# Attention of a two-layer hybrid step: unsplit probabilities, an fp32 product with the values stationary, two heads in the halves of the array

## The chip, the cores and the metric

The kernel runs on one core of a Trainium2 chip. The metric is the device time of one execution in microseconds (us); each time given for a kernel is the median of several executions. The traces come from one profiled execution.

## What is computed

One step of a two-layer hybrid model over 640 tokens: 512 latent tokens (four tiles of 128) and 128 context tokens (one tile). Each layer has an input projection, an attention beside two smaller branches, an output projection and a mixture of experts. The part at issue is the attention:

```python
def block_attention(q, k, v):
    # H = 8 query heads, KV = 2 key/value heads, G = 4 query heads per key head, Dh = 64
    ...
    def one_block(qblk):
        s = jnp.einsum('bqkgd,bmkd->bkgqm', qblk, k).astype(jnp.float32) * scale
        p = jax.nn.softmax(s, axis=-1).astype(v.dtype)
        return jnp.einsum('bkgqm,bmkd->bqkgd', p, v)
    ...
```

Everything is fp32. Latent queries read 640 keys (four tiles of latent keys and one tile of cached keys), context queries read the 128 context keys. After the attention each of the three branches gets an RMS norm of its own; the merged 1024 columns go into the output projection.

## The kernel before

The kernel is written engine by engine, with every wait and its count by hand. Matrix products of full accuracy are made of fp32r (reduced fp32) parts: a tensor is split into a high part (a copy rounded to fp32r, on ScalarE) and a low part (the difference, on VectorE), and products of parts are accumulated.

The attention of a layer is one loop of 40 steps u = 8t + h: t runs over five token tiles in the order context, latent 0 to 3 (`ORDER`), h over eight heads. Tile t = 0 has one block of 128 keys, the others have five. TensorE in step u does, in this order:

1. the scores of head u: two products each (query parts against key parts) for 512 and 128 keys, into one of two PSUM slots (banks 0 and 1, or 2 and 3; L1421, L1422), once the exponentials of head u-2 are read out;
2. five transpositions of the probabilities of head u-1 into banks 4 and 5, of which there is one copy only (L1432), once the exponentials of u-1 are there and VectorE has read the transposed probabilities of u-2;
3. the product of head u-2 with the values into bank 6 (L1444 and L1446): for each block of keys the transposed high part of the probabilities (stationary, 128x128) against the value's two parts side by side (128 columns), then the low part against the value's high part (64 columns);
4. in the first two steps of a tile, transpositions of the next tile's queries (L1400), and in the steps that `ADA_AT` names (u = 10 to 15 and 26 to 31; two units in each of u = 10, 11, 26, 27, else one) a unit of the modulation's matrix product: four fp32 products with 32 stationary columns each, one in each quarter of the array's columns, 512 columns moving (L1314), whose weights come by a DMA of 1 MB into a ring of four.

ScalarE in step u copies the high part of the transposed probabilities of u-1 (`pTH`, L750), then takes the exponentials of u with their row sums (L758). VectorE takes the negated maximum of the scores of u (L1055) and then the low part of the transposed probabilities of u-1 (`pTL`, L1060). After every fourth head `o_low` (ScalarE, L723) and `o_high` (VectorE, L1032, L1033, L1036) add the two halves of the product and multiply by the reciprocal row sums; bank 6 is free for the next four heads when L1033 is done. Ahead of the loop the values of all six key tiles are split into `vv` (two copies on ScalarE, two subtractions on VectorE).

Other work that shares these engines: `split_hi` / `split_lo` of a projection weight in step 36; `branch_squares` (ScalarE, L737) and `normalise` (VectorE, L1044) of a finished token tile; `piece_add` (VectorE, L905) after the eighth and the sixteenth modulation unit, that is in steps 15 and 31. GpSimd first runs the convolution (six 128x1280 operations, L505 to L510), then `piece_out` (four small stores, L481), the loads of the next bias (L474), and `branch_stats` of the context tile (L516 to L518), on which `normalise(0)` waits in step 16.

Of the kernel before, what the change touches and what calls it, by code (L numbers as in the profile page):

```python
# [53 lines left out]
for _l in range(DEPTH):  # L54
# [15 lines left out]
    "v_hi": NKV, "v_lo": NKV, "k_hi": NKV, "k_lo": NKV, "kT_psum": NKEY, "kk": NKEY,  # L70
    "q_hi": NT, "q_lo": NT, "qT_psum": 2 * NT, "qT": 2 * NT, "scores": NT * NH, "nmax": NT * NH, "prob": NT * NH,
    "pT_psum": NT * NH, "pT_hi": NT * NH, "pT_lo": NT * NH, "pv": NT * NH, "o_low": 2 * NT, "o_read": 2 * NT,
    "attn_done": 2 * NT, "ss3": 3 * NT, "rstd3": NT, "mrg_ready": 3 * NT, "mT_psum": KD, "mT_hi": 2 * KD, "mT_lo": 2 * KD,
# [11 lines left out]
def build(nc, I, O):  # L85
    with ExitStack() as ctx:
# [86 lines left out]
        junk3 = pool[:, 11776:12288]  # L173
# [13 lines left out]
        piece = [misc[:, 0:N], frow[:, 0:N], frow[:, 0:N]]  # L187
        bpiece = [misc[:, N:2 * N], frow[:, N:2 * N], frow[:, N:2 * N]]
# [57 lines left out]
        def at(name, l, n):  # L246

            return l * PER_LAYER[name] + n
# [191 lines left out]
        def _(pl):  # L440
# [49 lines left out]
            for l in range(DEPTH):  # L490
# [10 lines left out]
                bias_in(l, 1)  # L501
# [32 lines left out]
                for t in range(3, NT):  # L534
                    branch_stats(t)

# [61 lines left out]
        def _(act):  # L598
# [27 lines left out]
            for l in range(DEPTH):  # L626
# [81 lines left out]
                for v in range(NKV):  # L708
                    act.activation(vv[v][:, :, 0:HD], kv[:, :, P + HD * v:P + HD * (v + 1)], ACT.Copy).then_inc(sem("v_hi"), 1)
# [9 lines left out]
                def o_low(g):  # L719

                    t, r = divmod(g, 2)
                    act.wait_ge(sem("pv"), at("pv", l, 4 * g + 4))
# [930 lines left out]
```

## Time and profile before

| | before |
|---|---|
| median of 3 runs (lowest, highest) | 1258.35 us (1257.8, 1263.3) |
| the profiled execution, its own time | 1263.37 us |
| its span, first to last instruction | 1261.4 us |
| attention of layer 1 of 2, first score to last normalised head | about 168 to 299 us of the span |
| attention of layer 2 of 2 | about 770 to 913 us |
| TensorE busy over the span | 1011.3 us (80%) |
| VectorE, ScalarE, GpSimd busy | 725.7, 609.4, 280.4 us |
| mean granted TensorE clock | 0.859 of 2.4 GHz |

TensorE's rows are matmuls (PE) and weight loads (PEld), which overlap; an fp32 product that is not fp32r shows as two weight loads and two matmuls. Where several matmuls stand as one row, "x5" is the number of their records. A granted clock of 1.00 is 2.4 GHz, 0.50 is 1.2 GHz.

### The profile page before, as it was taken

The page shows a single profiled execution, that of the slowest core. Times are in us where ns is not written, and L with a number is a line of the kernel's source. Part 1 is how long each engine was busy: PE and PEld are TensorE (multiplying, and loading weights), DVE is VectorE, ACT ScalarE, POOL GpSimd, SP SyncE. Part 2 cuts the span into 40 slices and gives each one's busy share as a digit, 9 for nine tenths or more (in the row PEclk, how much of TensorE's full clock was granted, in tenths as well). Part 3 has the DMA queues.
Part 4 walks back from the last instruction along what each step waited for, and adds up shares of the span by engine and source line. Part 5 has one row for each costly group of instructions (what it writes and reads, how often), then busy time and mean ns, then how long its engine had stood idle before and what let it go on. Part 6 is the DMA issues. An engine that isn't in the chain of part 4 may idle for free.

```text
span 1261.4 us, 14900 instructions
## 1 busy us (share of the span) xinstructions
PE 1011.3 (80%) x5192; PEld 816.4 (65%) x5192; DVE 725.7 (58%) x952; ACT 609.4 (48%) x904; POOL 280.4 (22%) x312
## 2 busy tenths in 40 slices
PE   3899978997988299998169997999889636999930
PEld 0588866876765078886148886787777535888720
DVE  0367055664434669997446704555533765999826
ACT  1652254654211168897265225544521224988822
POOL 3032052010241112120413305101002502112023
PEclk9999979996995589999569997959789657999965
DMA  9954018271316659998742301716213225999933
GB/s 329 282 213 161 8 46 293 79 256 56 121 67 235 231 211 404 418 413 294 258 165 70 113 30 46 273 54 245 90 34 117 87 96 198 395 411 419 372 134 153
DMA packets 85950, 248.33 MB, mean 197 GB/s; under 512 B 25644, under 2 KB 30252, under 8 KB 75656
## 3 DMA queue, kind: packets, MB, share of 16 engines
q1 hardware_dynamic: 72760, 209.54, 44.8%
q0 software_dynamic: 11696, 32.84, 7.6%
q10 hardware_dynamic: 1440, 5.24, 1.0%
q8 instruction: 32, 0.52, 0.2%
q14 instruction: 22, 0.18, 0.0%
HBM read 221.05 MB, written 30.21 MB: 199 GB/s over the span
## 4 chain that ended last, share of the span: by engine, by line
PE 65%; DVE 11%; DMA 9%; ACT 6%; issue 5%; POOL 4%; SPq 0%; POOLq 0%; ACTq 0%; DVEq 0%
PE ps L1297 11%; PE ps L1299 11%; PE ps L1298 10%; DMA pool<-in_moe_w 4%; PE ps L1304 4%; PE ps L1306 3%; PE ps L1305 3%; PE ps L1432 3%; PE ps L1444 3%; PE ps L1314 3%; PE ps L1446 2%; PE ps L1522 2%; PE ps L1421 2%; PE ps L1550 2%; PE ps L1422 2%
## 5 line engine op out<-in xcount | busy, mean ns | idle before, releaser
L1297 PE MATMUL ps<-wH,actH 128*128 128x512 f32 x608 | 248.5, 409 | 16.2 <-DVE actL L1245 12.0
L1299 PE MATMUL ps<-wH,actL 128*128 128x512 f32 x608 | 241.8, 398 | 0.0
L1298 PE MATMUL ps<-wL,actH 128*128 128x512 f32 x608 | 241.3, 397 | 0.0
L1165 DVE TENSOR_TENSOR wL<-raw,wH 128x2048 fp32r<-128x2048 f32 x64 | 146.0, 2284 | 11.3 <-ACT wH L804 10.6
L1297 PEld LDWEIGHTS ps<-wH,actH 128*128 128x128 f32 x608 | 117.5, 193 | 41.8 <-issue 13.3
L1299 PEld LDWEIGHTS ps<-wH,actL 128*128 128x128 f32 x608 | 116.8, 192 | 26.0
L1298 PEld LDWEIGHTS ps<-wL,actH 128*128 128x128 f32 x608 | 117.4, 193 | 22.9
L804 ACT ACTIVATE wH<-raw 128x2048 fp32r<-128x2048 f32 x64 | 122.0, 1910 | 4.1 <-DMA raw<-in_moe_w 4.1
L1304 PE MATMUL ps<-wH,actH 128*128 128x512 f32 x256 | 105.0, 410 | 4.7 <-DVE wL L1165 3.3
L1306 PE MATMUL ps<-wH,actL 128*128 128x512 f32 x256 | 101.4, 396 | 0.0
L1305 PE MATMUL ps<-wL,actH 128*128 128x512 f32 x256 | 101.1, 395 | 0.0
L565 POOL DMA_INDIRECT pool<-h2s,idxc x32 | 56.0, 1750 | 198.6 <-PE ps L1550 165.9
L750 ACT ACTIVATE actH<-ps 128x640 fp32r<-128x640 f32 (+1 forms) x80 | 49.5, 618 | 92.0 <-PE ps L1432 91.8
L1165 DVE TENSOR_TENSOR wL<-pool,wH 128x2048 fp32r<-128x2048 f32 x32 | 73.1, 2285 | 21.5 <-ACT wH L804 21.5
L1055 DVE TENSOR_REDUCE nmax<-ps 128x1 f32<-128x640 f32 (+1 forms) x80 | 57.1, 714 | 49.0 <-PE ps L1422 48.2
L1060 DVE TENSOR_TENSOR actL<-ps,actH 128x640 fp32r<-128x640 f32 (+1 forms) x80 | 57.2, 715 | 39.3 <-ACT actH L750 39.3
L1432 PE MATMUL ps<-ident,pool 128*128 128x128 f32 x336 | 62.0, 316 | 21.5 <-ACT pool L758 19.2
L1314 PE MATMUL ps<-raw,cpad 128*32 128x512 f32 x384 | 60.8, 731 | 21.8 <-DMA raw<-in_w_ada 21.8
L758 ACT ACTIVATE pool<-ps,nmax 128x640 f32<-128x640 f32 (+1 forms) x80 | 56.4, 705 | 25.3 <-DVE nmax L1055 25.1
L932 DVE TENSOR_TENSOR wL<-raw,wH 128x2048 fp32r<-128x2048 f32 x24 | 54.6, 2290 | 23.5 <-ACT wH L632 23.3
L819 ACT ACTIVATE actH<-ps 128x512 fp32r<-128x512 f32 x64 | 38.3, 598 | 56.4 <-PE ps L1550 53.9
L632 ACT ACTIVATE wH<-raw 128x2048 fp32r<-128x2048 f32 x24 | 45.9, 1931 | 38.4 <-PE ps L1299 38.4
(222 smaller groups left out, 1952.5 us busy)
## 6 DMA issues: line engine op xcount, KB each, us to landing
raw<-in_w_ada SPq DMA_DIRECT2D x48, 1024.0 KB, 6.7
raw<-in_moe_w SPq DMA_DIRECT2D x96, 512.0 KB, 7.4
raw<-in_w_in SPq DMA_DIRECT2D x16, 1024.0 KB, 8.4
raw<-in_moe_w SPq DMA_DIRECT2D x16, 1024.0 KB, 11.8
pool<-in_moe_w SPq DMA_DIRECT2D x32, 512.0 KB, 7.4
pool<-in_moe_w SPq DMA_DIRECT2D x16, 1024.0 KB, 10.4
ys<-pool SPq DMA_DIRECT2D x32, 512.0 KB, 10.7
pool<-modrow POOLq DMA_DIRECT2D x16, 512.0 KB, 5.1
```

What stands on the lines that cost most here:

```text
L804: act.activation(wH[:, i, :], mraw[parity][i], ACT.Copy).then_inc(sem(f"m_hi{i}"), 1)
L1055: dve.tensor_reduce(nmax[:, u % 2:u % 2 + 1], flat[:, 2 * N * (u % 2):2 * N * (u % 2) + keys], X, ALU.max, negate=True).then_inc(sem("nmax ...
L1060: dve.tensor_tensor(pTL[:, v % 2, 0:keys], flat[:, 4 * N:4 * N + keys], f32(pTH[:, v % 2, 0:keys]), ALU.subtract).then_inc(sem("pT_lo"), 1)
L1165: dve.tensor_tensor(wL[:, i, :], mraw[parity][i], f32(wH[:, i, :]), ALU.subtract).then_inc(sem(f"m_lo{i}"), 1)
L1297: pe.matmul(out, aH, wH[:, slot_, cols_], start=first, stop=False)
L1298: pe.matmul(out, aH, wL[:, slot_, cols_], start=False, stop=False)
L1299: return pe.matmul(out, aL, wH[:, slot_, cols_], start=False, stop=last)
L1304: pe.matmul(out, aH, hi, start=first, stop=False)
L1305: pe.matmul(out, aH, lo, start=False, stop=False)
L1306: return pe.matmul(out, aL, hi, start=False, stop=last)
L1314: m = pe.matmul(ps[32 * j:32 * j + 32, ada_bank(l, q), :], c32, raw[:, POS["ada", l, n] % RAWS, j * N:(j + 1) * N], start=(kt == 0), stop= ...
L1432: m = pe.transpose(ps[:, 4 + c // 4, (c % 4) * P:(c % 4) * P + P], prob[:, w % 2, c * P:(c + 1) * P], ident[:, :])
```

## The change

The probabilities are no longer split, and neither are the values. Heads are handled in pairs: step 2p handles head p' of the first key head and step 2p+1 the corresponding head of the second. The transposed probabilities of the even head are copied from PSUM by ScalarE, those of the odd head by VectorE, both in fp32 into `pT` (two buffers, one of them where the rotary tables were). In odd steps TensorE forms the product of a whole pair in fp32: the values are stationary (64 columns), the transposed probabilities move (128 columns), the first head's result goes to partitions 0 to 63 and the second's to 64 to 127 of bank 6. The result is the transposed output of two heads; ScalarE copies it out (`oT_out`), TensorE transposes it back into another part of bank 6 in the next even step, ahead of the transpositions of the probabilities, and VectorE multiplies it by the reciprocal row sums on its way to `mrg` (`pair_out`). `o_low`, `o_high` and the split of the values go.

Buffers move: `junk3`, `piece`, `bpiece` go into parts of `aux`. So on GpSimd `bias_in(l, 1)` waits for the end of the convolution and stands behind it, and the loads of `n2row` and of the first gate (`grow`) go from the middle of the attention to its end, the latter behind a wait for the last pair.

```diff
-        pTH = actH[:, 3072:4352].rearrange("p (b n) -> p b n", b=2)
-        pTL = actL[:, 3072:4352].rearrange("p (b n) -> p b n", b=2)
-        vv = [t[:, 4352:5120].rearrange("p (j n) -> p j n", j=NKEY) for t in (actH, actL)]
+        pT = [t.rearrange("p (v n) -> p v n", v=NKV) for t in (pool[:, 5120:6400], tabs[:, :, :, :, :].rearrange("p t a b d -> p (t a b d)"))]
+        oT = [pool[:, c:c + P] for c in (11520, 11648)]
...
                 if q == 1:
-                    pl.wait_ge(sem("k_final"), at("k_final", l, NT))
+                    pl.wait_ge(sem("conv_done"), at("conv_done", l, 1))
...
-                bias_in(l, 1)
                 tap = lambda w: cw[:, w, :].unsqueeze(1).to_broadcast([P, NT, 256])
...
+                bias_in(l, 1)
                 piece_out(l, 1)
                 bias_in(l, 2)
                 branch_stats(0)
-                pl.wait_ge(sem("conv_done"), at("conv_done", l, 1))
-                pl.dma_start(n2row, row(I["norm2"][l])).then_inc(sem("norm2_row"), 16)
-                pl.wait_ge(sem("piece_out"), at("piece_out", l, 64))
-                for c in range(2):
-                    pl.dma_start(grow[:, c, :], row(modrow[l][c, 2 * D:3 * D])).then_inc(sem("gate1_row"), 16)
...
                 for t in range(3, NT):
                     branch_stats(t)
+                pl.dma_start(n2row, row(I["norm2"][l])).then_inc(sem("norm2_row"), 16)
+                pl.wait_ge(sem("attn_done"), at("attn_done", l, 4 * NT))
+                for c in range(2):
+                    pl.dma_start(grow[:, c, :], row(modrow[l][c, 2 * D:3 * D])).then_inc(sem("gate1_row"), 16)
...
+                def oT_out(p):
+
+                    act.wait_ge(sem("pv"), at("pv", l, p + 1))
+                    if p >= 2:
+                        act.wait_ge(sem("oT_psum"), at("oT_psum", l, p - 1))
+                    act.activation(oT[p % 2], ps[:, 6, 0:P], ACT.Copy).then_inc(sem("oT"), 1)
...
-                for u in range(NT * NH + 1):
-                    if u >= 1:
-                        v = u - 1
-                        keys = 5 * P if v >= NH else P
-                        act.wait_ge(sem("pT_psum"), at("pT_psum", l, v + 1))
-                        if v >= 2:
-                            act.wait_ge(sem("pv"), at("pv", l, v - 1))
-                        act.activation(pTH[:, v % 2, 0:keys], flat[:, 4 * N:4 * N + keys],
-                                       ACT.Copy).then_inc(sem("pT_hi"), 1)
+                for u in range(NT * NH + 3):
+                    if u % 2 and u < NT * NH:
+
+                        w = u - 1
+                        keys = 5 * P if w >= NH else P
+                        act.wait_ge(sem("pT_psum"), at("pT_psum", l, w + 1))
+                        if w >= 4:
+                            act.wait_ge(sem("pv"), at("pv", l, w // 2 - 1))
+                        act.activation(pT[w // 2 % 2][:, 0, 0:keys], flat[:, 4 * N:4 * N + keys], ACT.Copy).then_inc(sem("pT"), 1)
+                    elif u % 2 == 0 and u >= 4:
+                        oT_out(u // 2 - 2)
...
+                def pair_out(p):
+
+                    t, r = divmod(p, 4)
+                    dst = mrg[:, ORDER[t], 0:512].rearrange("p (v r d) -> p v r d", v=NKV, r=4)[:, :, r, :]
+                    dve.wait_ge(sem("oT_psum"), at("oT_psum", l, p + 1))
+                    c = 2 * p % 16
+                    link(dve.reciprocal(rinv[:, 2 * r:2 * r + 2], rsum[:, c:c + 2]))
+                    dve.tensor_tensor(dst, ps[:, 6, P:2 * P].rearrange("p (v d) -> p v d", v=NKV), bc(rinv[:, 2 * r:2 * r + 2], HD),
+                                      ALU.mult).then_inc(sem("attn_done"), 1)
...
-                    if u >= 1:
-                        v = u - 1
-                        keys = 5 * P if v >= NH else P
-                        dve.wait_ge(sem("pT_hi"), at("pT_hi", l, v + 1))
-                        dve.tensor_tensor(pTL[:, v % 2, 0:keys], flat[:, 4 * N:4 * N + keys],
-                                          f32(pTH[:, v % 2, 0:keys]), ALU.subtract).then_inc(sem("pT_lo"), 1)
-                    if u >= 2 and (u - 2) % 4 == 3:
-                        o_high((u - 2) // 4)
+                    if u % 2 == 0 and 2 <= u <= NT * NH:
+
+                        w = u - 1
+                        keys = 5 * P if w >= NH else P
+                        dve.wait_ge(sem("pT_psum"), at("pT_psum", l, w + 1))
+                        if w >= 4:
+                            dve.wait_ge(sem("pv"), at("pv", l, w // 2 - 1))
+                        dve.tensor_copy(pT[w // 2 % 2][:, 1, 0:keys], flat[:, 4 * N:4 * N + keys]).then_inc(sem("pT"), 1)
+                    if u % 2 == 0 and u >= 4:
+                        pair_out(u // 2 - 2)
...
+                    if u % 2 == 0 and u >= 4:
+                        p = u // 2 - 2
+                        pe.wait_ge(sem("oT"), at("oT", l, p + 1))
+                        pe.transpose(ps[:, 6, P:2 * P], oT[p % 2], ident[:, :]).then_inc(sem("oT_psum"), 1)
...
-                    if u >= 2:
-
-                        w = u - 2
-                        t, h = divmod(w, NH)
-                        pe.wait_ge(sem("pT_lo"), at("pT_lo", l, w + 1))
-                        if w % 4 == 0 and w:
-                            pe.wait_ge(sem("o_read"), at("o_read", l, w // 4))
-                        slots = range(5) if t else [CTXK]
-                        o = (h % 4) * P
+                    if u % 2 and u >= 3:
+
+                        p = (u - 3) // 2
+                        pe.wait_ge(sem("pT"), at("pT", l, 2 * p + 2))
+                        if p:
+                            pe.wait_ge(sem("attn_done"), at("attn_done", l, p))
+                        slots = range(5) if p >= 4 else [CTXK]
                         for c, j in enumerate(slots):
-                            pe.matmul(ps[:, 6, o:o + P], pTH[:, w % 2, c * P:(c + 1) * P], vv[h // 4][:, j, :],
-                                      start=(c == 0), stop=False, skip_group_check=True)
-                            m = pe.matmul(ps[:, 6, o:o + HD], pTL[:, w % 2, c * P:(c + 1) * P], vv[h // 4][:, j, 0:HD],
-                                          start=False, stop=(c == len(slots) - 1), skip_group_check=True)
+                            for v in range(NKV):
+                                m = pe.matmul(ps[HD * v:HD * v + HD, 6, 0:P], kv[:, j, P + HD * v:P + HD * (v + 1)], pT[p % 2][:, v, c * P:(c + 1) * P],
+                                              start=(c == 0), stop=(c == len(slots) - 1))
                         m.then_inc(sem("pv"), 1)
```

## Rows read from the trace of the kernel before

**Rows 1.** The page: span; shares of the chain that ended last, by engine.

```profile
span 1261.4 us, 14900 instructions
PE 65%; DVE 11%; DMA 9%; ACT 6%; issue 5%; POOL 4%; SPq 0%; POOLq 0%; ACTq 0%; DVEq 0%
```

**Rows 2.** Windows: stretch, length, busy of PE PEld DVE ACT POOL, clock, DMA, GB/s.

```profile
168.00:186.00 18.00, 13.35 (x56) 11.63 (x57) 9.49 (x22) 9.78 (x33) 16.87 (x6) 0.53 0.02 4
190.00:211.00 21.00, 21.00 (x169) 14.06 (x169) 11.47 (x17) 10.94 (x26) 0.00 (x0) 1.00 0.86 315
815.00:852.00 37.00, 33.70 (x168) 32.00 (x168) 17.67 (x29) 17.09 (x38) 7.54 (x16) 0.62 0.25 84
```

**Rows 3.** Chain of waits, attention: start, length, what, number of records.

```profile
190.90 1.85 PE ps L1314 x16
...
201.33 0.57 PE ps L1432 x5
202.94 0.99 PE ps L1314 x8
...
204.77 0.57 PE ps L1432 x5
...
831.39 1.09 PE ps L1432 x5
...
835.78 1.09 PE ps L1432 x5
```

**Rows 4.** Timeline of one step with a modulation unit: start, length, engine, line.

```profile
200.43 0.19 PEld L1421 LDWEIGHTS ps<-actH,actL 128*128 128x128 f32 x1 [0.84 <-ACT pool L758]
...
201.13 0.53 PEld L1432 LDWEIGHTS ps<-ident,pool 128*128 128x128 f32 x5
201.36 0.82 DVE L1055 TENSOR_REDUCE nmax<-ps 128x1 f32<-128x640 f32 x1 [1.30 <-PE ps L1422]
201.63 0.19 PEld L1444 LDWEIGHTS ps<-actH 128*128 128x128 f32 x1
...
202.86 0.16 PEld L1314 LDWEIGHTS ps<-raw,cpad 128*32 128x32 f32 x8
```

**Rows 5.** Timeline of a step without one, at the full clock.

```profile
229.42 0.82 DVE L1060 TENSOR_TENSOR actL<-ps,actH 128x640 fp32r<-128x640 f32 x1 [0.49 <-ACT actH L750]
...
230.36 0.53 PEld L1432 LDWEIGHTS ps<-ident,pool 128*128 128x128 f32 x5
...
231.16 0.70 ACT L750 ACTIVATE actH<-ps 128x640 fp32r<-128x640 f32 x1 [1.00 <-PE ps L1432]
...
231.76 0.79 ACT L758 ACTIVATE pool<-ps,nmax 128x640 f32<-128x640 f32 x1
...
231.90 0.82 DVE L1060 TENSOR_TENSOR actL<-ps,actH 128x640 fp32r<-128x640 f32 x1 [0.64 <-ACT actH L750]
...
232.44 0.20 ACT L758 ACTIVATION_READ_ACCUMULATOR pool<-ps,nmax 128x1 f32 x1
```

**Rows 6.** Chain of waits: a full-accuracy fp32 product, 320 moving columns (two records).

```profile
163.63 0.54 PE ps L1390 x2
```

**Rows 7.** Groups of instructions, shapes apart: the nearest small ones.

```profile
L750 ACT ACTIVATE actH<-ps 128x128 fp32r<-128x128 f32 x16 | 4.4, 277 | 6.7 <-PE ps L1432 6.6
L1032 DVE RECIPROCAL rinv<-rsum 128x4 f32<-128x4 f32 x20 | 3.6, 178 | 10.2 <-ACT pool L723 10.2
```

**Rows 8.** Timeline: the same VectorE operation during the convolution and after it.

```profile
179.67 1.91 DVE L1036 TENSOR_TENSOR pool<-pool,rinv 128x256 f32<-128x256 f32 x1
...
204.39 0.42 DVE L1036 TENSOR_TENSOR pool<-pool,rinv 128x256 f32<-128x256 f32 x1
```

**Rows 9.** Timeline: VectorE's wait in step 16 for GpSimd.

```profile
217.48 1.01 DVE L1044 TENSOR_SCALAR pool<-pool,stat 128x512 f32<-128x512 f32 x3 [3.65 <-POOL stat L518]
```

**Rows 10.** Chain of waits: the last head's transpositions and the last output.

```profile
293.05 0.76 PE ps L1432 x5
...
298.91 0.44 DVE pool L1036
```

More of the change, by code:

```diff
@@ L69 @@
     "z_done": NT, "shifted": 96, "conv_done": 1, "front_used": 1, "sgT_psum": 1, "sgT_ready": 1, "sgu_psum": 4, "sgu_done": 4,
[L70 removed]
+    "k_hi": NKV, "k_lo": NKV, "kT_psum": NKEY, "kk": NKEY,
     "q_hi": NT, "q_lo": NT, "qT_psum": 2 * NT, "qT": 2 * NT, "scores": NT * NH, "nmax": NT * NH, "prob": NT * NH,
[L72 to L73 removed]
+    "pT_psum": NT * NH, "pT": NT * NH, "pv": 4 * NT, "oT": 4 * NT, "oT_psum": 4 * NT,
+    "attn_done": 4 * NT, "ss3": 3 * NT, "rstd3": NT, "mrg_ready": 3 * NT, "mT_psum": KD, "mT_hi": 2 * KD, "mT_lo": 2 * KD,
     "gate1_row": 32, "scale2_row": 32, "shift2_row": 32, "gate2_row": 32, "oproj_psum": 2 * NT, "oproj": 2 * NT,
@@ L759, in _ @@
                             accum_out=rsum[:, u % 16:u % 16 + 1]).then_inc(sem("prob"), 1)
-                    if u >= 2 and (u - 2) % 4 == 3:
-                        o_low((u - 2) // 4)
                     if u in W_AT:
@@ L774, in _ @@
                             q_hi(t + 2)
-                o_low(2 * NT - 1)
                 branch_squares(NT - 1)
@@ L1007, in _ @@
                                           ).then_inc(sem("z_done"), 1)
-                for v in range(NKV):
-                    dve.wait_ge(sem("v_hi"), at("v_hi", l, v + 1))
-                    dve.tensor_tensor(vv[v][:, :, HD:], kv[:, :, P + HD * v:P + HD * (v + 1)], f32(vv[v][:, :, 0:HD]),
-                                      ALU.subtract).then_inc(sem("v_lo"), 1)
                 def sgu_out(g):
@@ L1023, in _ @@
                     sgu_out(g)
-                def o_high(g):
-                    t, r = divmod(g, 2)
-                    dst = mrg[:, ORDER[t], 256 * r:256 * r + 256].rearrange("p (h d) -> p h d", h=4)
-                    dve.wait_ge(sem("o_low"), at("o_low", l, g + 1))
-                    c = (8 * t + 4 * r) % 16
-                    link(dve.reciprocal(rinv[:, 4 * r:4 * r + 4], rsum[:, c:c + 4]))
-                    dve.tensor_tensor(dst, ps[:, 6, :].rearrange("p (h s d) -> p h s d", h=4, s=2)[:, :, 0, :], dst,
-                                      ALU.add).then_inc(sem("o_read"), 1)
-                    dve.wait_ge(sem("o_read"), at("o_read", l, g + 1))
-                    dve.tensor_tensor(dst, dst, bc(rinv[:, 4 * r:4 * r + 4], HD), ALU.mult).then_inc(sem("attn_done"), 1)
+                def pair_out(p):
[6 more added lines that the diff above has]
+                                      ALU.mult).then_inc(sem("attn_done"), 1)
                 def normalise(t):
                     dve.wait_ge(sem("rstd3"), at("rstd3", l, t + 1))
-                    dve.wait_ge(sem("attn_done"), at("attn_done", l, 2 * t + 2))
+                    dve.wait_ge(sem("attn_done"), at("attn_done", l, 4 * t + 4))
                     for j, (a, b) in enumerate(((0, 512), (512, 768), (768, 1024))):
@@ L1047, in _ @@
                 q_lo(1)
-                for u in range(NT * NH + 1):
+                for u in range(NT * NH + 3):
                     if u < NT * NH:
@@ L1073, in _ @@
                         piece_add(l, 1 + PIECE_AT.index(u))
-                o_high(2 * NT - 1)
                 normalise(NT - 1)
@@ L1406, in _ @@
                 pe.wait_ge(sem("kk"), at("kk", l, NKEY))
-                pe.wait_ge(sem("v_lo"), at("v_lo", l, NKV))
+                pe.wait_ge(sem("kv_raw"), at("kv_raw", l, NT))
                 pe.wait_ge(sem("sgu_done"), at("sgu_done", l, 4))
-                for u in range(NT * NH + 2):
+                for u in range(NT * NH + 3):
                     if u < NT * NH:
-                        t, h = divmod(u, NH)
-                        v = h // 4
-                        if h == 0:
+                        t, s_ = divmod(u, NH)
+                        v, h = s_ % 2, s_ // 2 + 4 * (s_ % 2)
+                        if s_ == 0:
                             pe.wait_ge(sem("qT"), at("qT", l, 2 * t + 2))
```

21 lines of the change are left out of this document (6 added, 15 removed).

## The prediction

> **What bounds the kernel now.** I read the page first, then the granted clock and busy time of stretches of the attention, then the chain of waits, then single steps in the timeline. TensorE holds 65% of the chain that ended last [rows 1]. The change touches only the attention loops, some 131 us and 143 us long, so the question is what bounds a step there. There are three answers.
>
> Steps with a modulation unit (u = 10 to 15 and 26 to 31): TensorE is busy 21.00 of 21.00 us at the full clock [rows 2], and the transpositions of successive steps start 204.77 - 201.33 = 3.44 us apart [rows 3]. The weight loads mark one step [rows 4]: scores 200.43 to 201.13, 0.70 us; transpositions to 201.63, 0.50; product with the values to 202.86, 1.23; the unit 0.99 [rows 3]. The sum is 3.42: TensorE has no slack.
>
> Steps without one, at the full clock: these follow a loop through three engines. The transpositions start at 230.36, ScalarE's high copy at 231.16, VectorE's low part at 231.90; it lasts 0.82 and the next transpositions wait for it, as those at 230.36 did for the low part of 229.42 to 230.24 [rows 5]. That is 0.80 + 0.74 + 0.82 + about 0.1 = 2.46 us, just above TensorE's own 0.70 + 0.50 + 1.23 at most.
>
> Steps at the lower clock: in layer 2, 815 to 852, the clock is 0.62 on average, TensorE is busy 33.70 of 37.00 us [rows 2], and steps are 835.78 - 831.39 = 4.39 apart [rows 3]: TensorE again.
>
> **Part by part**, per pair of latent heads, with a full-clock row unless said.
>
> Product. Before: 2 x 1.23 = 2.46. It has 5 x (128 + 64) x 2 = 1920 columns, 0.80 us at 2.4 GHz, so columns are not its price; its 20 matmuls each wait for a 128-column load, some 0.11 apart. The new one has ten fp32 products of 128 columns. An fp32 product of 320 columns takes 0.54 us [rows 6], which is 4.05 cycles a column at 2.4 GHz, so one of 128 takes 0.213. Whether the two halves run side by side the trace shows in quarters: a second modulation unit adds 1.85 - 0.99 = 0.86 [rows 3] for four products of 512 columns, where one alone would take 4 x 512 / 2.4 = 0.853. Four ran in the time of one, and their weight loads vanish behind them. So the pair takes 5 x 0.213 = 1.07. What one unit takes beyond 0.86 is 0.13, the change into and out of the split array; I add it once. Taken: 1.2, with 0.05 for the next loads, 1.25. Bounds: 1.07 from the same rows, and 10 x 0.213 + 0.13 = 2.26 if the halves queue. I take the low side because the quarters are the same mechanism.
>
> The Trainium skill (TensorEngine Tiling (Array Packing), Key Properties) says that changing the tiling mode drains TensorE. It speaks against the change, which adds two mode changes per pair; the unit's 0.13 agrees with it. By that rule, with 0.13 due at each of the two, 32 pairs give back 4 us more than by one; the page has no figure of its own.
>
> Back-transposition: one matmul like the five that take 0.50 [rows 4], so 0.10, taken as 0.15; bounds 0.1 and 0.9, the latter if TensorE sits through the copy (0.28 like L750's 128x128 [rows 7], plus its latencies). In a step with a unit the copy is hidden by unit and scores (1.7 us), in others by the scores alone (0.70).
>
> VectorE: two low parts of 0.82 become one copy of the same 640 elements, 0.82 by L1060 [rows 5]; `pair_out` is a reciprocal of 0.18 and a product of some 0.28 [rows 7], as much per pair as `o_high` was. VectorE has 2 x 0.82 + 0.82 + 0.5 = 3.0 of work per pair. ScalarE: two high copies become one of 0.70 and one of 0.28. Neither engine bounds.
>
> Pairs with units: 2 x 0.70 + 2 x 0.50 + 1.25 + 0.15 + 2 x 0.99 = 5.78 against 6.88, 1.10 less. Six such pairs a layer, 12 in all: **13 us**.
>
> Pairs without, at the full clock. The old loop goes; late next is a longer one: exponentials 0.88 [rows 5] + 0.05, transpositions 0.50, pair product 1.25, scores of the next even head until their maximum starts 0.93 (200.43 to 201.36 [rows 4]), maximum 0.82 + 0.04: 4.47 against 4.9, or 5.2 with the 0.6 that `o_low` and `o_high` add to each fourth step. Two other paths tie with it: VectorE's copy of the odd head frees banks 4 and 5, and its `pair_out` frees bank 6, within 0.1 us of need. Ties seldom line up, so I take 4.7 and 0.5 a pair, bounds 0 and 0.75. Of the 20 pairs without units, 8 ran like this by the spacing of L1432 in the chain (six in layer 1, two in layer 2): **4 us**.
>
> Pairs at the lower clock, another 8, six of them in layer 2: a step takes 4.39 [rows 3] where TensorE's parts at the full clock sum to 2.40, a factor of 1.83; the new pair's 2 x 1.20 + 1.25 + 0.15 = 3.80 becomes 6.95, which I take as 7.2 against 8.78, and 1.4 won after ties: **11 us**. The last 4 are held in steps 16 and 36 by waits that stay (below): 0.5 each, **2 us**.
>
> Context tile: one block of keys, lower clock (0.53 [rows 2]); product and copies shrink little and two stages join, so 0, bounds -2 and +2. One thing is won: L1036, both inputs in SBUF, took 1.91 instead of 0.42 while GpSimd ran the convolution [rows 8]; `pair_out` reads PSUM, like L1055, which did not stretch. **3 us** in two layers.
>
> Tail: from the last transpositions at 293.05 to the end of the last output, 298.91 + 0.44, are 6.3 us [rows 10]. After: 0.8, VectorE's copy 0.83, the product 2.3, copy, back-transposition and `pair_out` 1.3: 5.3. **2 us** in two layers.
>
> At nothing: the split of the values, since the last score keys and queries came later (cover: TensorE's transpositions of keys; without it some 2 us a layer). On GpSimd `bias_in(1)` moves behind the convolution, 2 us of issue and one landing: its reader is `piece_add` in step 15, over 20 us later. `piece_out`, `bias_in(2)` and `branch_stats(0)` keep their order, so VectorE's wait of 3.65 us in step 16 [rows 9] stays. The second-norm and gate loads move to the end of the attention, behind `branch_stats` of the last tile; their readers come after a whole projection half, 30 us on. Uncovered, they would cost some 5 us a layer. Modulation weights arrive at 315 GB/s with the DMA busy 0.86 [rows 2]; a faster step asks for 1 MB per 2.9 us instead of 3.44, 360 GB/s, where 315 / 0.86 gives 366: it just fits, with four units ahead in the ring.
>
> Sum: 13 + 4 + 11 + 2 + 3 + 2 = 35. The 0.13 for the split array may fall due on the way in and on the way out, which is 4 us more in 32 pairs; I take off half of that: 33. The profiled execution took 1263.4 (span 1261.4 and 2 around it), so it would take 1230; the median shown is 5 lower, and I forecast **1225**, by itself 1215 to 1237.
>
> **Rivals.**
> - The clock rises sooner. Layer 2's second latent tile ran at the lower clock for most of its length [rows 2, 3], layer 1's at the full one by 229 us [rows 5], after the same stall; the new product keeps TensorE on columns rather than on weight loads. Four or five pairs at 4.7 instead of 7.2: 11 us more, 1214.
> - The clock stays low through both tiles without units, in both layers, because TensorE waits more often. Six pairs at 5.2 become 7.2 instead of 4.7: 15 us lost, 1240.
> - The round trip is exposed: TensorE stands in order behind ScalarE's copy in each even step, 0.6 a pair in 32 pairs, 19 us: 1244. For it speaks that ScalarE does the copy only after the odd head's exponentials; against it, the scores between.
> - Slower: the halves take turns, so the change doesn't do what it says. Then a pair's product is 2.26: 1.07 more in each of 32 latent pairs and twice that in the 12 at the lower clock, so 32 + 12 = 44 times 1.07 is 47, less some 4 where TensorE has slack in the loop, 43: 1268. It decides where 44 times the surplus is 33, at a product of 1.25 + 0.75 = 2.0 us. Against it stand the quarters of rows 3. The Trainium skill (FP8 and Floating Point Precision, TensorE Precision Notes) gives true fp32 as four passes through the array, which the 4.05 cycles a column agree with; it says nothing on halves.
>
> **How the numbers follow.** Chances: forecast 0.47, sooner clock 0.15, low clock 0.14, exposed round trip 0.10, halves in turn 0.14. A difference of 0.5%, 6.3 us, is about what a measurement here can tell from none. Faster: 0.47 + 0.15 + 0.09 + 0.05 = 0.76; within: 0.05 + 0.05 + 0.01 = 0.11; slower 0.13. The range leaves out the halves in turn and little else: 1207 to 1254.
>
> **What would show it.** Right: pair products in which the two halves start within 0.05 us of one another and that last 1.1 to 1.3 us at the full clock; pairs with units 5.7 to 6.0 apart; no TensorE wait for `oT` above 0.2 us; L1036's 1.9 us gone. Wrong: a product of 2 us or more, or modulation steps bound by DMA. The sum is wrong too if the stall of step 16 grows by what the steps before it save, or if the granted clock of the tiles without units differs from that of before.

## The result, and the profile after

| | before | after |
|---|---|---|
| median (lowest, highest), side by side | 1260.82 us (1257.8, 1267.8) | 1221.21 us (1219.96, 1224.83) |
| ratio of the medians, 95% interval | | 0.9683 [0.9634, 0.9732] |
| the profiled execution, its own time | 1263.37 us | 1220.32 us |
| its span; mean granted clock | 1261.4 us; 0.859 | 1218.5 us; 0.886 |

The forecast was 1225 us, in a range of 1207 to 1254: the time lies 3.8 us under the forecast. The profiled executions differ by 43.0 us. The table below takes the attention of each layer apart at the first exponential of each token tile; the last column ends with `normalise` of the last tile, some 4.4 us behind the last head's output. Tiles latent 0 and latent 2 hold the modulation units, latent 1 and 3 have none.

| us | context | latent 0 | latent 1 | latent 2 | latent 3 to end | sum |
|---|---|---|---|---|---|---|
| before, layer 1 | 15.4 | 27.6 | 27.5 | 28.0 | 35.4 | 133.8 |
| before, layer 2 | 15.4 | 28.6 | **35.4** | 30.2 | 36.1 | 145.7 |
| after, layer 1 | 13.9 | 25.3 | 24.9 | 26.2 | 31.0 | 121.3 |
| after, layer 2 | 13.9 | 25.7 | 25.1 | 26.2 | 30.9 | 121.7 |

So 36.5 of the 43.0 us are in the attention, 10.3 of them in one tile. Another 6.5 lie where no code changed: from the start of the last `h2` ahead of layer 1's router to the cast of the router's index lists it takes 32.8 us before and 26.3 after (called the router stage below). The first question is therefore whether these two places belong to the change at all.

The chain of waits of the kernel after, a pair of heads with modulation units (start, length, what, records); it answers to [rows 3]. L1436 is the new product, L1303 a unit, L1425 the transpositions of the probabilities.

```profile
197.99 1.24 PE ps L1436 x20
199.23 0.99 PE ps L1303 x8
...
201.19 0.55 PE ps L1425 x5
201.74 0.99 PE ps L1303 x8
...
204.14 1.24 PE ps L1436 x20
```

The product of two heads takes 1.24 us, the pair 204.14 - 197.99 = 6.15 where it took 6.88. The timeline of TensorE's weight loads in the same stretch (start, length, engine, line, shapes, idle time just before in brackets) shows what the 1.24 consists of; it answers to [rows 4]:

```profile
200.86 0.14 PEld L1416 LDWEIGHTS ps<-ident,pool 128*128 128x128 f32 x1
200.92 0.58 PEld L1425 LDWEIGHTS ps<-ident,pool 128*128 128x128 f32 x5
201.67 0.16 PEld L1303 LDWEIGHTS ps<-raw,cpad 128*32 128x32 f32 x8 [0.17 <-issue]
...
203.37 0.53 PEld L1425 LDWEIGHTS ps<-ident,pool 128*128 128x128 f32 x5
204.06 1.07 PEld L1436 LDWEIGHTS ps<-pool 128*64 128x64 f32 x20 [0.17 <-issue]
205.31 0.16 PEld L1303 LDWEIGHTS ps<-raw,cpad 128*32 128x32 f32 x8 [0.17 <-issue]
```

The loads of the pair's twenty matmuls (ten fp32 products, two records each) take 1.07 us, the forecast's figure to the digit. What stands beside it is the 0.17 in brackets: each time the array goes into another form (whole to halves at 204.06, halves to quarters at 205.31, whole to quarters at 201.67) the loads stand still for 0.17 us, three times in a pair with units.

By the loads, the pair is two scores of 0.70, transpositions of 0.69 and 0.75 with the gap behind them, the product of 1.25 with the gap behind it, a back-transposition of 0.06 and two units of 0.99: 6.13 in sum.

### The profile page after: what moved, and what is told of

It is laid out like the page before. It is cut to its first block, busy times and chain, and to the rows that moved or that the text cites. A ratio compares the mean times of both kernels' runs of the same rounds, so it can differ in the third digit from the quotient of the medians.

```text
span 1218.5 us, 14984 instructions
## 1 busy us (share of the span) xinstructions
PE 960.8 (79%) x5232; PEld 753.8 (62%) x5232; DVE 686.8 (56%) x928; ACT 585.6 (48%) x880; POOL 282.5 (23%) x312
## 4 chain that ended last, share of the span: by engine, by line
PE 59%; DVE 13%; DMA 11%; ACT 7%; issue 5%; POOL 4%; SPq 1%; POOLq 0%; ACTq 0%; DVEq 0%
PE ps L1286 11%; PE ps L1288 11%; PE ps L1287 10%; PE ps L1293 3%; PE ps L1295 3%; PE ps L1294 3%; PE ps L1303 3%; PE ps L1425 3%; DMA raw<-in_moe_w 3%; DMA pool<-in_moe_w 3%; PE ps L1436 2%; PE ps L1410 2%; ACT wH L799 2%; DVE wL L1154 1%; PE ps L1540 1%
## 5 line engine op out<-in xcount | busy, mean ns | idle before, releaser
L1286 PE MATMUL ps<-wH,actH 128*128 128x512 f32 x608 | 248.2, 408 | 17.3 <-DVE actL L1234 13.2
L1303 PE MATMUL ps<-raw,cpad 128*32 128x512 f32 x384 | 57.8, 697 | 21.8 <-DMA raw<-in_w_ada 21.8
L799 ACT ACTIVATE wH<-pool 128x2048 fp32r<-128x2048 f32 x32 | 61.2, 1911 | 4.8 <-DMA pool<-in_moe_w 4.8
L1540 PE MATMUL ps<-ident,pool 128*128 128x128 f32 x256 | 39.9, 282 | 29.0 <-DMA pool<-h2s,idxc 29.0
L1425 PE MATMUL ps<-ident,pool 128*128 128x128 f32 x336 | 57.3, 299 | 6.1 <-ACT pool L756 4.9
```

Of the source, the lines that this page charges most:

```text
L799: act.activation(wH[:, i, :], mraw[parity][i], ACT.Copy).then_inc(sem(f"m_hi{i}"), 1)
L1286: pe.matmul(out, aH, wH[:, slot_, cols_], start=first, stop=False)
L1303: m = pe.matmul(ps[32 * j:32 * j + 32, ada_bank(l, q), :], c32, raw[:, POS["ada", l, n] % RAWS, j * N:(j + 1) * N], start=(kt == 0), stop= ...
L1425: m = pe.transpose(ps[:, 4 + c // 4, (c % 4) * P:(c % 4) * P + P], prob[:, w % 2, c * P:(c + 1) * P], ident[:, :])
```

## The experiments

**Do the halves run side by side?** The first kernel issues all products of one half before those of the other:

```diff
-                        for c, j in enumerate(slots):
-                            for v in range(NKV):
+                        for v in range(NKV):
+                            for c, j in enumerate(slots):
```

> The changed kernel with the ten fp32 products of a pair in another order: all five of the first half, then all five of the second, so that neighbours share a half of the array and can't run side by side. Nothing else differs. Theory (the gain is TensorE's time for the product, and it hangs on the two halves running together): a pair's product goes from 1.24 to about 2.2 us at the full clock, each of 32 latent pairs gets about 1 us longer, and the time rises from 1221 to 1250 to 1262, which is the old kernel's. Rival (the gain is the shorter chain through ScalarE and VectorE, and the product lies beside it): under 10 us, at most 1231. Second rival (two products of one half overlap as well): no change.

Measured: 1245.32 us (1240.5 to 1249.57), ratio to before 0.9875 [0.9812, 0.9938]. Its chain of waits:

```profile
200.65 1.95 PE ps L1436 x20
202.60 0.99 PE ps L1303 x8
```

In turn the product takes 1.95 instead of 1.24, so the halves do run side by side in the changed kernel. The medians are 24.1 us apart, but not all of that is the product's: the attention tiles grew by 17.1 us in sum, and the router stage, whose code is the same, stood at 33.2 instead of 26.3. The 0.71 would be 23 us in 32 latent pairs; the pairs that are held at steps 16 and 36 did not get longer (in layer 1 their products start 10.23 and 8.62 us behind those ahead, against 10.46 and 8.90). The time is under the range expected for this reason, and because the product in turn takes 1.95 and not about 2.2: why products of one half take less than their sum is open.

**What does the back-transposition cost where it stands?** Here it is moved behind the transpositions of the probabilities:

```diff
-                    if u % 2 == 0 and u >= 4:
-                        p = u // 2 - 2
-                        pe.wait_ge(sem("oT"), at("oT", l, p + 1))
-                        pe.transpose(ps[:, 6, P:2 * P], oT[p % 2], ident[:, :]).then_inc(sem("oT_psum"), 1)
                     if 1 <= u <= NT * NH:
...
                         m.then_inc(sem("pT_psum"), 1)
+                    if u % 2 == 0 and u >= 4:
+                        p = u // 2 - 2
+                        pe.wait_ge(sem("oT"), at("oT", l, p + 1))
+                        pe.transpose(ps[:, 6, P:2 * P], oT[p % 2], ident[:, :]).then_inc(sem("oT_psum"), 1)
```

> The changed kernel with the back-transposition of a pair behind the transpositions of the probabilities in TensorE's order, instead of ahead of them. Theory: TensorE's waits for ScalarE's copy (23 us in 16 waits in the trace of the changed kernel) lie mostly where TensorE waits for VectorE or GpSimd anyway, and only some 0.1 to 0.2 us in pairs without units are lost: 1216 to 1221. Rival (the round trip is exposed, 0.6 us a pair): 1200 to 1206. If the pair's output gets late instead, so that the next product waits for bank 6: slower, up to 1230.

Measured: 1214.98 us (1212.86 to 1218.12), ratio 0.9648 [0.9593, 0.9702]: 6.2 us less than the changed kernel, just under what the theory expected. The changed kernel was not run beside it and the two ratios' intervals overlap, but no execution of the one (1219.96 and up) reaches the other's, and in the traces the attention fell from 243.0 to 235.7 us in sum. The waits of TensorE in the changed kernel, 190 to 240 us, say where (waiter, releaser, us in total, times, longest):

```profile
PE ps L1416 <- ACT pool L721: 4.9, 3, 4.2
```

and its chain where step 16 has been held:

```profile
214.05 0.74 DVE nmax L1043
...
216.08 0.29 ACT pool L721
216.41 0.48 PE ps L1416
216.89 1.07 PE ps L1425 x5
```

In a step that is held, the exponentials come late, ScalarE's copy of the product comes behind them, and TensorE stands before the back-transposition although the probabilities are there: from the maximum at 214.05 to the transpositions at 216.89 it takes 2.84 us. With the block moved, this is 1.70:

```profile
215.10 0.74 DVE nmax L1043
...
216.80 1.30 PE ps L1421 x5
```

(L1421 is the same transposition there.) In steps that run freely nothing changed: pairs with units are 6.15 apart in both kernels (198.97 to 205.12 with the block moved), pairs without 4.68 and 4.67 (224.59 to 229.27, and 224.41 to 229.08). The tiles say the same: latent 1 went from 24.9 and 25.1 to 23.7 and 23.4, latent 3 from 31.0 and 30.9 to 30.0 and 30.1, latent 2 fell by 0.8 and the context tile by 0.4 in each layer, latent 0 rose by 0.3 in one layer and fell by 0.5 in the other.

**The stall of step 16 and the clock.** In both kernels step 16 waits for `normalise(0)`, and that for GpSimd, which first does four stores and four loads:

```profile
206.44 0.70 DVE pool L900
...
207.42 2.01 POOL modrow L481 x4
209.50 2.02 POOL pool L474 x4
212.13 0.88 POOL stat L517
213.44 0.61 DVE pool L1032 x2
```

(chain of the kernel after). From the end of `piece_add` to the last two of the three operations of `normalise(0)` are 213.44 - 207.14 = 6.3 us, as they were before (211.58 to 217.88). Two kernels take this away by doing `branch_stats(0)` ahead of `piece_out(l, 1)` and `bias_in(l, 2)`, one made from the kernel before, one from the kernel after:

```diff
+                branch_stats(0)
                 piece_out(l, 1)
                 bias_in(l, 2)
-                branch_stats(0)
```

> The kernel before with one line moved on GpSimd: the statistics of the context tile ahead of the small stores and loads of the modulation, which removes VectorE's wait of 3.65 us in step 16 and with it TensorE's longest idle time in the attention. Theory (the granted clock falls in that idle time, and in layer 2 of the kernel before it stayed low for the whole next tile): the second latent tile of layer 2 falls from 35.4 us to about 23, that of layer 1 from 27.5 to 22, in all 15 to 18 us: 1243 to 1246. Rival (the clock of that tile has other causes than this stall): only the stall itself goes, 6 to 8 us: 1253 to 1255.

> The changed kernel with the same line moved. Theory: the stall is 3.5 to 4 us a layer here too, and a few us at the lower clock behind it go as well: 1209 to 1214. Against the kernel before with the line moved this gives the worth of the change without the help of the clock: if 10 us of the change's 40 were the clock of one tile, the two kernels with the moved line lie about 30 apart; if the clock had no part, about 40.

Measured: 1244.12 us (1240.17 to 1250.63), ratio 0.9884 [0.9819, 0.995], and 1214.08 us (1212.03 to 1216.21), ratio 0.9634 [0.9579, 0.9689]. They are 30.0 us apart, as expected if the clock has a part, where the kernels before and after are 39.6 apart. The granted clock of latent 1 in windows (stretch, length, busy of PE PEld DVE ACT POOL, clock, DMA share, GB/s), first the kernel before, layer 2, then the kernel before with the statistics first, layer 1:

```profile
820.00:824.00 4.00, 1.14 (x8) 0.94 (x9) 3.44 (x9) 2.25 (x5) 1.53 (x3) 0.99 0.53 181
824.00:850.00 26.00, 26.00 (x115) 24.84 (x114) 12.10 (x17) 10.90 (x26) 1.25 (x3) 0.50 0.11 37
```

```profile
218.00:222.00 4.00, 3.97 (x34) 3.67 (x32) 3.23 (x6) 2.81 (x5) 1.06 (x2) 1.00 0.47 158
222.00:226.00 4.00, 3.62 (x28) 3.20 (x27) 2.75 (x5) 2.37 (x5) 0.00 (x0) 1.00 0.79 266
```

TensorE is busy 1.14 of 4 us in the stall, then the clock is at its lower level (1.2 GHz) although it is busy all the time. Without the stall the clock stays at 2.4 GHz throughout latent 1, and this tile takes 22.1 us in both layers of the one, 19.3 in both of the other. The attention takes 130.3 and 129.2 us against 117.5 and 117.7: the change is worth 24.3 us in the attention when neither kernel meets the stall of step 16. A second stall, in step 36, stays in both, and the clock falls behind it in both (0.50 over 282 to 296 us of the one and 269 to 275 of the other, layer 1), so latent 3 is not free of the clock in this comparison.

**Does the lower clock belong to the kernel?** Both kernels once more, unaltered, for their traces:

> The kernel before once more, for its trace alone. If the granted clock goes with the kernel: second latent tile 27.5 us in layer 1 and 35.4 in layer 2, router stage of layer 1 32.8 us. If it differs between executions of one kernel: the second latent tile of layer 2 at 26 to 28 us, or that of layer 1 at 35, and a router stage of 27 us can come.

> The changed kernel once more, for its trace alone. If the granted clock goes with the kernel: attention tiles within 0.3 us of the first trace (layer 1 13.9, 25.3, 24.9, 26.2, 31.0; layer 2 13.9, 25.7, 25.1, 26.2, 30.9) and the router stage of layer 1 (last h2 to the lists) 26.3 us. If it differs between executions of one kernel: second latent tile of one layer up to 33 us, router stage 33 us.

Measured, one execution each: 1251.28 us and 1224.05 us, 27.2 apart where the first traces are 43.0 apart. The kernel before, the same code, has 29.6 us in latent 1 of layer 1 (27.5 in the first trace) and **26.65** in layer 2 (35.4), and 27.0 in the router stage (32.8). Its windows in layer 2:

```profile
817.00:821.00 4.00, 0.96 (x8) 0.78 (x7) 2.63 (x6) 1.35 (x4) 2.02 (x4) 1.00 0.48 158
821.00:825.00 4.00, 3.73 (x21) 3.33 (x20) 3.19 (x7) 2.40 (x5) 0.51 (x1) 0.67 0.77 261
825.00:829.00 4.00, 4.00 (x32) 3.87 (x31) 2.23 (x4) 2.23 (x5) 0.00 (x0) 0.91 0.03 12
```

The same stall, the same work, and the clock is at its lower level for some 3.4 us (8 us x (0.33 + 0.09)) instead of some 30 us, from 824 to about 854. The four traced stalls of the kernel before order the tile by this stretch: some 3.4 us low go with 26.65 us in latent 1, 6.8 with 27.5, 10.2 with 29.6 and 30 with 35.4. The layers of one execution differ as much as the executions do. So how long the lower clock lasts is not fixed by the code. The kernel after repeated itself: all tiles within 0.4 us of the first trace, the router stage 27.3 us. In its windows (first trace, layer 1) the clock falls too, and stays low for some 6.8 us, as it does in both layers of both its traces:

```profile
213.00:217.00 4.00, 0.59 (x3) 0.59 (x4) 2.48 (x5) 2.18 (x6) 0.01 (x1) 0.66 0.11 36
217.00:221.00 4.00, 4.00 (x22) 3.48 (x22) 2.52 (x5) 1.35 (x5) 0.00 (x0) 0.50 0.02 4
221.00:225.00 4.00, 3.48 (x34) 2.98 (x31) 2.17 (x5) 1.95 (x6) 0.00 (x0) 0.99 0.00 0
```

The router stage swings with the granted clock too. Its logits' products in the two traces of the kernel before (timeline: start, length, engine, line, shapes; below them the window of 21 us around them), first trace, then second:

```profile
392.49 3.60 PE L1522 MATMUL ps<-rw,pool 128*128 128x20 f32 x16
399.67 3.60 PE L1522 MATMUL ps<-rw,pool 128*128 128x20 f32 x16
...
384.00:405.00 21.00, 18.30 (x95) 13.82 (x91) 11.98 (x6) 2.83 (x3) 1.00 (x2) 0.57 0.79 273
```

```profile
395.15 2.19 PE L1522 MATMUL ps<-rw,pool 128*128 128x20 f32 x16
399.18 1.96 PE L1522 MATMUL ps<-rw,pool 128*128 128x20 f32 x16
...
387.00:408.00 21.00, 20.31 (x136) 15.56 (x136) 12.47 (x9) 3.50 (x4) 0.64 (x2) 0.74 0.91 306
```

Over all traces of this study the stage of layer 1 took between 26.3 and 33.2 us, with the same code there; variants of the kernel after met the long one too. The Trainium skill (TensorE: Matmul & The Clock Gate, Part 1) says that the gate's window runs free of the kernel, and that the number of products at the lower clock when a kernel starts therefore varies between runs of one kernel. That 35.4 and 26.65 us stand for the same tile agrees with it in kind; the sentence speaks of the start of a kernel, and why one stretch lasted 30 us no run here shows.

**How much of the old time was the low part?** The kernel before, without the products of the low part of the probabilities; the low part itself is still computed and waited for:

```diff
                             pe.matmul(ps[:, 6, o:o + P], pTH[:, w % 2, c * P:(c + 1) * P], vv[h // 4][:, j, :],
...
-                            m = pe.matmul(ps[:, 6, o:o + HD], pTL[:, w % 2, c * P:(c + 1) * P], vv[h // 4][:, j, 0:HD],
```

> The kernel before without the five products of the low part of the probabilities per head (64 columns each): that part of the output is left out, the low part itself is still computed and waited for. TensorE's share of a head's product falls from about 1.23 to 0.7 us, nearly what the change saves on TensorE (2.46 to 1.24 a pair), while VectorE's chain and the waits stay. Theory (where TensorE has no slack its time is the gain; elsewhere the chain is): the steps with a modulation unit go from 3.44 to about 2.9 and 24 of them give 12 to 13 us, steps without one at the full clock stay at 2.46, those at the lower clock fall from 4.39 to about 3.9: 1238 to 1246 in all. Rival (TensorE's time is all of it): as much as the change, 1218 to 1226.

Measured: 1229.78 us (1229.0 to 1231.44), ratio 0.9745 [0.9708, 0.9781], between the two cases. Tiles with units fell by 3.3 to 3.4 us each against the second trace of the kernel before, 13.4 in sum, where 12 to 13 were expected; latent 1 of layer 1 fell from 27.5 in the first trace, with a stretch at the lower clock as long, to 27.15 only. Where TensorE bounds the step the product counts, where the loop of the two copies bounds it, it doesn't. That is the theory's picture. Its 1238 to 1246 was missed by 8 us: latent 1 of layer 2 stood at 26.5 instead of the first trace's 35.4 and the router stage at 27.3 instead of 32.8, and these 14.4 us would bring it to 1244. With half the products left out a pair with units takes 2 x 2.91 = 5.82 (transpositions at 196.33, 199.24, 202.15); the change, with the whole product, takes 6.15.

**Three other arrangements of the pair.** The first puts the product into the even step behind the scores, ScalarE's copy behind its exponentials, and the back-transposition and `pair_out` into the next odd step; the second does this with the statistics first; the third leaves the product where it is and moves the modulation units from even into odd steps.

```diff
-                    if u % 2 and u >= 3:
+                    if u % 2 == 0 and u >= 4:
-                        p = (u - 3) // 2
+                        p = (u - 4) // 2
```

```diff
-none, third = (0,) * NH, (0, 0, 2, 2, 1, 1, 1, 1)
+none, third = (0,) * NH, (0, 0, 0, 4, 0, 2, 0, 2)
```

> The changed kernel with the product of a pair one step later, behind the scores of the next even head, the copy of its result behind that head's exponentials, the back-transposition and pair_out in the odd step after. It takes the product out of the loop that bounds pairs without units (exponentials, transpositions, product, scores, maximum). Theory: those pairs fall from about 4.7 us to TensorE's own time, 1.4 + 1.1 + 1.25 + 0.2 = 3.95, some 14 pairs, and the late back-transposition gives what it gave alone (6): 1203 to 1210. Rival (the two other paths that tie, VectorE's copy and pair_out, hold the pair at 4.5): 1213 to 1216, as with the late back-transposition alone. If the clock falls because TensorE now waits elsewhere: slower than 1221.

> The same with the statistics of the context tile ahead of the small stores on GpSimd as well, so without the stall of step 16. Theory: the two gains add, as they touch different tiles for the most part: 7 us below the kernel without that line, 1196 to 1203. Rival: with the shorter pairs the stall is what is left of several waits and going without it gives 10 or more; or the late product has already filled it, 0 to 3.

> The changed kernel with the modulation units of two steps put together behind a pair's product in the odd step (0, 0, 0, 4, 0, 2, 0, 2 for 0, 0, 2, 2, 1, 1, 1, 1), so that TensorE goes once less into and out of the split array in each pair with units; the number of units and of products is the same. Theory (each entry costs 0.17 us of idle weight loads and each leaving about 0.13): pairs with units go from 6.13 to about 5.85, 12 pairs, 3 to 4 us: 1217 to 1219. Rival (the entries are hidden): 1221. If the longer block of units delays the scores of the next head beyond what VectorE and ScalarE have in store: slower, 1224 or more.

Measured: 1224.27 us (1219.59 to 1230.23), 1216.97 (1216.64 to 1217.07) and 1229.15 (1228.23 to 1229.6). All three miss the ranges of their theories. The first won 4.6 us in the attention (238.4 against 243.0 in sum) and met 33.1 us in the router stage, so what puts its median above 1221 is not the attention, where its third case looked for it. The second lies 7.3 us under the first, the difference that was expected. In pairs without units its chain shows a new loop in place of the old:

```profile
219.96 1.31 PE ps L1422 x20
221.28 0.71 PE ps L1433 x5
222.01 0.84 DVE tabs L1051
222.98 0.75 PE ps L1433 x5
223.75 0.71 ACT pool L747
224.50 1.31 PE ps L1422 x20
```

(L1422 is the product there, L1433 the transpositions.) Banks 4 and 5 hold one head's transposed probabilities; with the product in between, transposition, copy, transposition, copy, product stand one behind the other, 4.54 us instead of 4.68. The scores have left the chain, and next to nothing is won. Its units, moreover, ran into their weights once:

```profile
188.35 7.00 DMA raw<-in_w_ada
```

The third came out in its slower case (1224 or more): it shows the price of a change of form and what avoiding it costs. Its chain:

```profile
199.73 1.24 PE ps L1436 x20
200.97 1.85 PE ps L1303 x16
...
203.69 0.83 DVE nmax L1043
...
206.25 1.24 PE ps L1436 x20
```

Two units in a row save one change (1.85 against 2 x 0.99), but the pair takes 6.52 instead of 6.15: behind product and both units the scores come late, and maximum, exponentials and transpositions follow them on the chain with TensorE idle. Spread over both steps, as in the change, the units cover that latency.

**Both gains together.** The changed kernel with the back-transposition moved and the statistics first:

> The changed kernel with both edits: the back-transposition behind the transpositions of the probabilities, and the statistics of the context tile ahead of the bias loads on GpSimd. Alone they gave 1221.2 - 1215.0 = 6.2 and 1221.2 - 1214.1 = 7.1 us. Theory: they are won in different places (6.2 in the pairs, 7.1 in step 16), so they add: 1206 to 1210, attention of a layer 113 to 115 us. Rival: both end in the same wait (a tile that comes sooner to step 16 only waits longer for GpSimd, or the clock rises later): 1211 to 1215, attention 116 to 118 us.

Measured: 1208.0 us (1206.08 to 1210.46), ratio to before 0.9596 [0.9539, 0.9652]. The attention takes 113.0 and 113.4 us, latent 1 is 19.1 in both layers, and the windows (latent 1 of layer 1) show why:

```profile
207.00:211.00 4.00, 3.91 (x40) 3.32 (x39) 3.12 (x8) 2.89 (x7) 3.80 (x8) 1.00 0.98 376
211.00:215.00 4.00, 3.48 (x35) 3.03 (x35) 3.01 (x6) 2.85 (x7) 0.03 (x1) 1.00 0.27 79
```

No stall in step 16, and no fall of the clock in latent 1; behind step 36 it still falls. The two gains of 6.2 and 7.1 by the medians add up to 13.2, as the theory had it. In the traces the attention fell by 16.5 us, where the two edits alone gave 7.3 and 7.7, and the router stage stood at 30.1. This version beats both kernels.

## Why the prediction was right, and where it was not

**The product: right.** 1.25 us were taken, 1.24 measured. The argument from the quarters in [rows 3] and the fp32 product in [rows 6] gave 1.07 for the loads of the pair, and 1.07 it is.

**The split form: mis-sized.** The step "What one unit takes beyond 0.86 is 0.13, the change into and out of the split array; I add it once" was wrong in number more than in size. The price is 0.17, and it falls due at each change of form that the trace shows a gap for: into the product, from product to unit, and from transpositions to unit in the even step, where the transpositions now come directly ahead of it. The transposition blocks therefore take 0.69 and 0.75 us by the loads, with the gap behind them (203.37 to 204.06, 200.92 to 201.67), and not 0.50. A pair with units takes 6.15, not 5.78; it won 0.73, not 1.10, which is 8.8 us in 12 pairs and not 13. The prediction weighed a second change at 4 us in all and took off half of that; the 0.37 in 12 pairs are 4.4. The Trainium skill (TensorEngine Tiling (Array Packing), Key Properties) says that changing the tiling mode drains TensorE; the idle 0.17 us at each change agrees with it.

**The back-transposition: right where TensorE runs freely, wrong where it is held.** It takes 0.06 of the loads' time in a unit step. But "no TensorE wait for `oT` above 0.2 us" failed: layer 1 has eight of them with 11.1 us, the longest 4.2, most of which TensorE would have stood in any case. What the place of the block costs is 6.2 us by the medians and 7.3 by the attention of the traces, in the experiment that moved it. The rival of an exposed round trip had the mechanism and put it in all 32 pairs at 19 us; it acts where something else has held a step.

**Pairs without units: right.** 4.7 at the full clock was taken, 4.68 measured, on the chain that was forecast (exponentials, transpositions, product, scores, maximum); others of layer 1 are 4.8 and 5.1 apart:

```profile
224.59 0.53 PEld L1425 LDWEIGHTS ps<-ident,pool 128*128 128x128 f32 x5 [0.67 <-ACT pool L756]
...
229.27 0.53 PEld L1425 LDWEIGHTS ps<-ident,pool 128*128 128x128 f32 x5 [0.66 <-ACT pool L756]
```

**Pairs at the lower clock: not what happened.** 11 us were to come from eight pairs that stay at the lower clock and need 7.2 instead of 8.78. In the traces after there is no run of such pairs: only the first pair behind the stall is at 1.2 GHz (its product 1.65 in layer 1). The tiles that had them won more, 10.3 us in latent 1 of layer 2 alone. But this is not the change's doing in the way that its product is: another execution of the kernel before had 26.65 us there. Where both kernels' clocks are nearer to each other behind the stall, layer 1 won 12.5 us (first traces, some 6.8 us low in both) and layer 2 134.8 - 121.4 = 13.4 (second traces, 3.4 low before and 6.8 after); without the stall they won 12.8 and 11.5. That is some 25 us in all. The medians differ by 39.6, so some 14 us are left; by the two places where the traces of one kernel differ, latent 1 and the router stage, they are the granted clock. This is a subtraction and not a measurement, since the other executions have no trace. The executions of the kernel before spread from 1251.28 to 1269.05 us over all runs, those of the kernel after from 1219.96 to 1224.83, which fits a stretch that varies in the one and not in the other; why is not settled. The rival "the clock rises sooner" had this mechanism at 11 us; that the new product has a part in it no run shows.

**The small terms: right.** Context tile: 3.1 us (15.4 to 13.9, twice) against 3; `pair_out` takes 0.29 during the convolution, where L1036 took 1.91 [rows 8]:

```profile
176.65 0.29 DVE L1023 TENSOR_TENSOR pool<-ps,rinv 128x128 f32<-128x128 f32 x1
```

Tail: from the last transpositions at 281.33 to the end of the last `pair_out`, 285.52 + 0.29, are 4.5 us; 5.3 were forecast and 6.3 before [rows 10]. The stall of step 16 stayed at 6.3 us. What was put at nothing, the loads moved on GpSimd and the transfers of the weights, appears nowhere on the chain of the attention; the units take 379 GB/s with the DMA busy 0.97, and TensorE is still busy 20.92 of 21 us [rows 2]:

```profile
190.00:211.00 21.00, 20.92 (x198) 13.72 (x197) 8.92 (x16) 10.31 (x26) 3.51 (x7) 1.00 0.97 379
```

That "just fits" was as narrow as it sounded: the kernel with the product half a pair later, whose units came at other moments, waited for their weights.

So the total came out within 3.8 us by luck, with two errors that nearly cancel: some 8 us too much in the parts that the change itself shortens (33 against 25), and 14 us of granted clock that the sum did not hold, on a forecast that also started 2.5 us lower, from the median of the first three executions. By the prediction's own signs the product was right (1.24 us, L1036's 1.9 us gone) and the sum was not: pairs with units are 6.15 apart and not 5.7 to 6.0, TensorE waits for `oT`, and the granted clock of the tiles without units differs from that of before.

## What to carry to other kernels

When products of small tiles are bound by their weight loads, putting two heads side by side in the array's halves pays, even in fp32; but count every change of the array's form, and group them where the latency behind allows it. Put a step that depends on another engine's late copy behind the work that is ready, not ahead of it: it costs nothing in free steps and shows only where something else has held the engine. Before a gain is credited to an edit, look whether the granted clock of unchanged stretches moved too, and trace the kernel before a second time.

## What was not expected of the hardware

TensorE stayed at 1.2 GHz over 824 to 850 us while its matmul rows filled 26.00 of 26.00 us, after a stall in which it was busy 1.14 of 4; in a second execution of the same kernel the clock behind this stall was back at 2.4 GHz after some 3.4 us. With it one tile differs by 8.8 us between two executions of one kernel, and the router stage by 5.8.

Two halves whose matmuls are issued in turn, one half's five products after the other's, took 1.95 us and not twice the 1.07 of the pair side by side.

A change of the array's form cost 0.17 us of idle weight loads, alike from whole to halves, halves to quarters and whole to quarters, and from halves back to whole (the scores behind a product without a unit):

```profile
226.53 0.19 PEld L1410 LDWEIGHTS ps<-actH,actL 128*128 128x128 f32 x1 [0.17 <-issue]
```

Behind a unit no such gap shows by itself: the loads of the next scores come 0.84 us behind the unit's own (205.47 to 206.30), while its matmuls still run.
